# Byte places of the matmul operands, and the order of two steps on POOL, in a hybrid encoder layer

## The chip, the cores and the metric

The kernel runs on one core of a Trainium2 chip. The metric is the device time of one execution in microseconds (us), median over runs. TensorE (PE) multiplies, ScalarE (ACT), VectorE (DVE) and GpSimd (POOL) compute elementwise, SyncE (SP) issues DMAs.

## What is computed

One layer over 512 tokens of width 1024: a half feed-forward block, a token mixer, a second half feed-forward block, each with a normalisation in front, then a last normalisation.

```python
x = x + 0.5 * g1 * swiglu(mod(rms_norm(x)), w1, w3, w2)      # 1024 -> 2816 -> 1024
h = mod(rms_norm(x)); z = h @ w_in                             # mixer: HGRN2 heads and RG-LRU blocks
x = x + g2 * concat(hgrn2(z), rglru(z)) @ w_out
x = x + 0.5 * g3 * swiglu(mod(rms_norm(x)), w1', w3', w2')
return rms_norm(x)
def swiglu(h, w1, w3, w2): return (silu(h @ w1) * (h @ w3)) @ w2
```

## The kernel before

Tokens lie transposed in SBUF, features on the partitions. Every float32 operand is split into an upper part (rounded to fp32r by ACT) and a lower part (the rest, by a subtraction on DVE), and each product is made of three matmuls: upper weights on upper tokens, upper weights on lower tokens, lower weights on upper tokens (`three`, and the loop in `product`). Upper weights are `whi`, lower ones `wlo`.

**Wide units.** A unit is 8 weight blocks of 128x128, 4 KB in each partition. SP loads it into `raw`, ACT copies it to `whi`, DVE subtracts into `wlo`. Each of its matmuls has 512 columns. The down projections of the feed-forward blocks run this way with tokens `ghi2`, `glo2`, and so do the mixer's projections, and the first 8 units of each feed-forward block (tokens `hhi`, `hlo`).

**Groups.** The other 18 of 22 column blocks of w1 and w3 are computed in 36 groups (18 in each feed-forward block, `PAIRS` = 9 times s = 0 and 1) by a Strassen-like scheme: instead of 8 block products there are 7 (`PRODUCTS`), each of 4 x 3 = 12 matmuls with 256 columns, so 84 matmuls per group. I number the groups g = 2j + s. Products 0, 5 and 6 read tokens `hhi`/`hlo`, products 1 to 4 sums of tokens kept in `forms`. Weights of products 0 to 3 are in `hi4`/`lo4`, which lie over `whi`/`wlo`; those of 4 to 6 in `hix`/`lox`.

The weights of a group come about like this:
- SP (`load_group`, L454) loads two quarters of the weights, each written twice, into `sraw_a[s]` ("base loads"; `sraw_a[1]` is `raw`), when DVE has subtracted the first two parts of group g-2. Then, when all four parts of g-2 are done, it loads a third quarter into `sraw_b[s]` (L457).
- POOL (`add_fourth`, L506) waits for the base loads and issues a DMA that adds the fourth quarter onto two of the four copies ("adding transfer").
- POOL (`long_sums`) waits for that DMA, adds `xs[0]` (L514), then `xs[1]` (L517).
- ACT (`group_upper`, L720) copies part 0, 1 (`sraw_a`), 2 (`xs`) and 3 (`sraw_b`) to the upper weights, each when TensorE has finished the products of the previous group that used this place.
- DVE (`group_lower`, L1377) subtracts in the same order. Part 1 also waits for the first sum of POOL, since its end frees `sraw_a` for SP's next load. Between the parts, in the fixed order of its queue, DVE evacuates the previous group's sums (L1385 to L1403) and multiplies the gates (L1410, L1412).
- TensorE (`product`, L1979 to L1981) waits for part 0 ahead of product 0, part 1 ahead of product 2, part 2 ahead of product 4, part 3 ahead of product 6.

POOL's queue is in order: adding transfer of g, sums of g, adding transfer of g+1, sums of g+1, and so on (`up_sums`).

**Places.** `sb` and `at` put tiles one behind the other, rounded to 64 bytes. The first tile begins at byte 16512 of each partition, which is 128 modulo 256. By the sizes of the tiles `hhi`, `hlo`, `raw`, `whi`, `wlo` begin at 128 modulo 256 too (and with them `hi4`, `lo4`, and `yhi`, `ylo` of the mixer), while `arena` and all that is counted from it (`ghi2`, `glo2`, `forms`, `hix`, `lox`, and the mixer's tiles) begin at 192. All strides inside a tile are multiples of 256 bytes, so the relation holds for each matmul.

Of the kernel before, what the change touches and what calls it, by code (L numbers as in the profile page):

```python
# [22 lines left out]
F32R = mybir.dt.float32r  # L23
# [4 lines left out]
P = 128  # L28
HALF = P // 2
T = 512  # L30
# [8 lines left out]
N_MOD = 9  # L39
EPS = 1e-6  # L40
UNIT = KD * P
HALF_UNITS = KF // 2
PAIR_UNITS = HALF_UNITS - 4
LEVELS = (64, 32, 16, 8, 4, 2, 1)
# [53 lines left out]
def build(nc, xt, wu, ws, wada, c_rows, vecs_in, bd_in, consts_in, out):  # L98
    with ExitStack() as ctx:
        place = [nc.sbuf_base + (-nc.sbuf_base) % 64]  # L100

        def at(name, shape, dt, offset):

            n = int(np.prod(shape[1:])) * (1 if dt == U8 else 4)
            return nc.alloc_sbuf_tensor_at(name, shape, dt, offset=offset), offset + (n + 63) // 64 * 64

        def sb(name, shape, dt=F32):
            t, place[0] = at(name, shape, dt, place[0])
            return t

        def sem(name):
            return ctx.enter_context(nc.semaphore(name))

# [3 lines left out]
        hhi = sb("hhi", [P, KD, T], F32R)  # L117
        hlo = sb("hlo", [P, KD, T], F32R)
        raw = sb("raw", [P, 2, UNIT])
        whi = sb("whi", [P, 2, UNIT], F32R)  # L120
        wlo = sb("wlo", [P, 2, UNIT], F32R)
        vecs = sb("vecs", [P, N_VEC])
        ident = sb("ident", [P, P])
        ones = sb("ones", [P, P])
# [11 lines left out]
        nomh, omk = small[:, 120:128], small[:, 128:136]  # L136
        half_b, half_gain = small[:, 56:72], small[:, 72:73]
        modt = sb("modt", [P, KD])
        arena = place[0]

        off = arena
        early, off = at("early", [P, BLOCKS, KD, T], F32, off)
        raw2, off = at("raw2", [P, 2, UNIT], F32, off)
# [5 lines left out]
        off = arena  # L149
        ghi2, _ = at("ghi2", [P, KF, T], F32R, off)  # L150
        forms, off = at("forms", [P, 4, 2, KD // 2 * HT], F32R, off + PLAIN * T * 4)
# [4 lines left out]
        csr, _ = at("csr", [P, D], F32, off - 4 * D)  # L156
        ada = tuple(at(f"ada{i}", [P, D], F32, a)[0] for i, a in
                    enumerate((off - 12 * D, off - 8 * D, off, off + 4 * D)))
        hix, off = at("hix", [P, 3, T], F32R, off)
        lox, off = at("lox", [P, 3, T], F32R, off)  # L160
        sraw_a = (sraw_a0, raw[:].rearrange("p u (q n) -> p (u q) n", q=2))
        sraw_b = (sraw_b0, sraw_b1)
        g2_at = off
        g2, off = at("g2", [P, KF, T], F32, g2_at)
        glo2, _ = at("glo2", [P, KF, T], F32R, g2_at)
        h32, t_at = at("h32", [P, KD, T], F32, g2_at + PLAIN * T * 4)
# [16 lines left out]
        off = arena  # L183
# [203 lines left out]

            return psum[:, 5 - 4 * s:7 - 4 * s, :].rearrange("p b (h t) -> p (b h) t", h=2)

        hi4 = whi[:].rearrange("p u (q n) -> p (u q) n", q=2)  # L390
        lo4 = wlo[:].rearrange("p u (q n) -> p (u q) n", q=2)
        h_left, h_right = h32[:, :, 0:HT], h32[:, :, HT:T]

        def tokens(i, k):
# [91 lines left out]
        def _(pool):  # L486
# [16 lines left out]
            def add_fourth(j, s):  # L503

                pool.wait_ge(base_loaded[s], 32 * j + 32)
                pool.dma_start(sraw_a[s][:, 1:3, :], twice(quarter(j, s, 3)), accum_op=ALU.add  # L506
                               ).then_inc(sum_loaded[s], 16)
# [11 lines left out]
            def up_sums(n):  # L519

                j0 = PAIRS * n
                add_fourth(j0, 0)
                long_sums(j0, 0)
                add_fourth(j0, 1)
                with pool.Fori(j0, j0 + PAIRS - 1) as j:
                    long_sums(j, 1)
                    add_fourth(j + 1, 0)
                    long_sums(j + 1, 0)
                    add_fourth(j + 1, 1)
                long_sums(j0 + PAIRS - 1, 1)  # L530

            def load_row(r):
# [50 lines left out]
        def _(act):  # L583
# [119 lines left out]
            def group_upper(j, s, part):  # L703

                if opens(j) and s == 0:
                    if part < 2:
                        act.wait_ge(unit_used, DOWN_AT[j // PAIRS] - 1 + part)
                else:
                    act.wait_ge(prod_done, 14 * j + (7 * s - (5, 3, 1, 0)[part]))
                if part == 3:  # L710
                    act.wait_ge(third_loaded[s], 16 * j + 16)
                if part < 2:
                    act.wait_ge(sum_loaded[s], 16 * j + 16)
                    src, dst = sraw_a[s][:, 2 * part:2 * part + 2, :], hi4[:, 2 * part:2 * part + 2, :]
                elif part == 2:
                    act.wait_ge(xs_done, 4 * j + (2 * s + 2))
                    src, dst = xs[:], hix[:, 0:2, :]
                else:
                    src, dst = sraw_b[s][:], hix[:, 2, :]
                nc.scalar.activation(dst, src, ACT.Copy).then_inc(shi_done, 1)  # L720
# [400 lines left out]
        def _(dve):  # L1121
# [244 lines left out]
            def group_lower(j, s, part):  # L1366

                dve.wait_ge(shi_done, 8 * j + (4 * s + part + 1))
                if part == 1:
                    dve.wait_ge(xs_done, 4 * j + (2 * s + 1))  # L1370
                if part < 2:
                    src, up, dst = (t[:, 2 * part:2 * part + 2, :] for t in (sraw_a[s], hi4, lo4))
                elif part == 2:
                    src, up, dst = xs[:], hix[:, 0:2, :], lox[:, 0:2, :]
                else:
                    src, up, dst = sraw_b[s][:], hix[:, 2, :], lox[:, 2, :]
                nc.vector.tensor_tensor(dst, src, up, ALU.subtract).then_inc(slo_done, 1)  # L1377
# [525 lines left out]
        def _(pe):  # L1903
# [48 lines left out]
            def product(j, s, i):  # L1952
# [19 lines left out]
                if i == 6:  # L1972
                    pe.wait_ge(p1_copied, 2 * j + (s + 1))
                dst = sum_bank(i, s)
                up, low = (hi4[:, i, :], lo4[:, i, :]) if i < 4 else (hix[:, i - 4, :], lox[:, i - 4, :])
                for k in range(KD // 2):
                    a, b = up[:, k * P:(k + 1) * P], low[:, k * P:(k + 1) * P]
                    rhi, rlo = tokens(i, k)
# [505 lines left out]
```

## Time and profile before

| | |
|---|---|
| median of 3 runs | 1018.17 us (1016.67 to 1020.95) |
| profiled execution | 1020.35 us |
| its span, first to last instruction | 1018.6 us |
| TensorE busy | 991.1 us |
| granted TensorE clock, mean | 0.997 |
| groups of the first feed-forward block | about 76 to 258 us |
| groups of the second | about 707 to 884 us |

The profile is one execution. Busy time of TensorE counts overlapping matmuls once; since matmuls are pipelined, the time that one costs is read from the distance between two starts, not from its length. Instructions that only wait or issue count as idle, except POOL's own issue of a DMA.

### The profile page before, as it was taken

How to read it: one execution, taken by the hardware profiler on the slowest of the kernel's cores; microseconds unless marked ns; L12 is line 12 of the kernel's file. 1: busy time of each engine (PE TensorE's matmuls, PEld its weight loads, DVE VectorE, ACT ScalarE, POOL GpSimd, SP SyncE). 2: the span in 40 equal slices, each digit the busy share in tenths (PEclk: the TensorE clock that was granted, in tenths of full speed). 3: DMA queues.
4: the chain of work that ended last, by engine and by line, in shares of the span. 5: the costliest groups of instructions: out<-in, count | busy, mean ns of one | idle time of the engine just before them, and what ended most of it. 6: DMA issues, size and time to landing. Idle time of an engine off the chain costs nothing.

```text
span 1018.6 us, 18633 instructions
## 1 busy us (share of the span) xinstructions
PE 991.1 (97%) x6974; PEld 862.8 (85%) x6974; DVE 751.4 (74%) x1039; ACT 502.9 (49%) x690; POOL 225.7 (22%) x191
## 2 busy tenths in 40 slices
PE   7999999999999999999999989999999999999997
PEld 5779999999888888776677767878999999988887
DVE  5777777887787858879899995566877877683334
ACT  5545444444333124588977973465444444433221
POOL 0023444453112301100100000202444443200100
PEclk9999999999999999999999999999999999999999
DMA  9556657665788736622221202235677676552322
GB/s 351 213 174 155 197 149 212 167 195 152 270 289 311 280 134 218 215 98 73 74 84 42 83 23 77 90 120 138 173 211 189 180 205 167 186 179 90 103 83 83
DMA packets 64470, 163.79 MB, mean 161 GB/s; under 512 B 5696, under 2 KB 8016, under 8 KB 64416
## 3 DMA queue, kind: packets, MB, share of 16 engines
q1 hardware_dynamic: 44720, 110.79, 30.6%
q0 software_dynamic: 18416, 50.16, 19.9%
q10 hardware_dynamic: 1280, 2.10, 0.9%
q8 instruction: 36, 0.59, 0.2%
q14 instruction: 18, 0.15, 0.0%
HBM read 158.83 MB, written 2.10 MB: 158 GB/s over the span
## 4 chain that ended last, share of the span: by engine, by line
PE 81%; DMA 5%; ACT 5%; DVE 5%; issue 2%; SPq 1%; DVEq 0%; POOLq 0%; ACTq 0%
PE psum L1907 15%; PE psum L1909 15%; PE psum L1908 14%; PE psum L1979 10%; PE psum L1981 10%; PE psum L1980 10%; DMA sraw_a<-ws 4%; DMA raw<-wu 1%; PE psum L2284 1%; PE psum L2278 1%; ACT whi L589 1%; PE psum L2208 1%; DVE wlo L1377 1%; PE psum L2210 1%; PE psum L2209 1%
## 5 line engine op out<-in xcount | busy, mean ns | idle before, releaser
L589 ACT ACTIVATE whi<-raw 128x1024 fp32r<-128x1024 f32 x92 | 97.3, 1057 | 221.1 <-PE psum L1909 209.5
L1125 DVE TENSOR_TENSOR wlo<-raw,whi 128x1024 fp32r<-128x1024 f32 x94 | 118.1, 1256 | 117.3 <-ACT whi L589 116.9
L1909 PE MATMUL psum<-ghi,wlo 128*128 128x512 f32 (+2 forms) x384 | 144.0, 375 | 0.0
L1908 PE MATMUL psum<-glo,whi 128*128 128x512 f32 (+2 forms) x384 | 143.3, 373 | 0.0
L1907 PE MATMUL psum<-ghi,whi 128*128 128x512 f32 (+2 forms) x384 | 143.2, 373 | 0.0
L1907 PE MATMUL psum<-hhi,whi 128*128 128x512 f32 x320 | 129.2, 404 | 2.0 <-DVE wlo L1125 1.3
L1909 PE MATMUL psum<-hhi,wlo 128*128 128x512 f32 x320 | 125.2, 391 | 0.0
L1908 PE MATMUL psum<-hlo,whi 128*128 128x512 f32 x320 | 125.0, 391 | 0.0
L1979 PE MATMUL psum<-forms,whi 128*128 128x256 f32 x432 | 121.2, 281 | 0.0
L1980 PE MATMUL psum<-forms,whi 128*128 128x256 f32 x432 | 120.7, 279 | 0.0
L1981 PE MATMUL psum<-forms,wlo 128*128 128x256 f32 x432 | 120.7, 279 | 0.0
L1377 DVE TENSOR_TENSOR wlo<-sraw_a,whi 128x1024 fp32r<-128x1024 f32 x36 | 56.7, 1594 | 48.8 <-ACT whi L720 47.4
L1908 PEld LDWEIGHTS psum<-glo,whi 128*128 128x128 f32 x384 | 72.1, 188 | 13.8
L1907 PEld LDWEIGHTS psum<-ghi,whi 128*128 128x128 f32 x384 | 72.2, 188 | 13.1
L1909 PEld LDWEIGHTS psum<-ghi,wlo 128*128 128x128 f32 x384 | 72.3, 188 | 12.2
L1981 PEld LDWEIGHTS psum<-forms,wlo 128*128 128x128 f32 x432 | 81.4, 188 | 0.0
L1979 PEld LDWEIGHTS psum<-forms,whi 128*128 128x128 f32 x432 | 81.3, 188 | 0.0
L1980 PEld LDWEIGHTS psum<-forms,whi 128*128 128x128 f32 x432 | 81.1, 188 | 0.0
L1979 PE MATMUL psum<-hhi,hix 128*128 128x256 f32 x288 | 80.0, 278 | 0.0
L1980 PE MATMUL psum<-hlo,hix 128*128 128x256 f32 x288 | 79.8, 277 | 0.0
L1981 PE MATMUL psum<-hhi,lox 128*128 128x256 f32 x288 | 79.8, 277 | 0.0
L1907 PEld LDWEIGHTS psum<-hhi,whi 128*128 128x128 f32 x320 | 60.1, 188 | 22.1 <-issue 5.5
(272 smaller groups left out, 2344.7 us busy)
## 6 DMA issues: line engine op xcount, KB each, us to landing
raw<-wu SPq DMA_DIRECT2D x96, 512.0 KB, 3.4
ada<-wada POOLq DMA_DIRECT2D x56, 512.0 KB, 5.1
sraw_a<-ws SPq DMA_DIRECT2D x36, 512.0 KB, 5.9
raw<-ws SPq DMA_DIRECT2D x36, 512.0 KB, 6.0
sraw_b<-ws SPq DMA_DIRECT2D x36, 256.0 KB, 4.3
sraw_a<-ws POOLq DMA_DIRECT2D x18, 512.0 KB, 6.1
raw<-ws POOLq DMA_DIRECT2D x18, 512.0 KB, 6.0
early<-wada SPq DMA_DIRECT2D x16, 512.0 KB, 15.3
```

The source lines that it names most:

```text
L589: nc.scalar.activation(whi[:, slot, :], raw[:, slot, :], ACT.Copy).then_inc(hi_done, 1)
L1125: nc.vector.tensor_tensor(wlo[:, slot, :], raw[:, slot, :], whi[:, slot, :], ALU.subtract).then_inc(lo_done, 1)
L1377: nc.vector.tensor_tensor(dst, src, up, ALU.subtract).then_inc(slo_done, 1)
L1907: nc.tensor.matmul(dst, a, rhi, start=start, stop=False)
L1908: nc.tensor.matmul(dst, a, rlo, start=False, stop=False)
L1909: return nc.tensor.matmul(dst, b, rhi, start=False, stop=stop)
L1979: nc.tensor.matmul(dst, a, rhi, start=(k == 0 and i < 6), stop=False, skip_group_check=(i == 6))
L1980: nc.tensor.matmul(dst, a, rlo, start=False, stop=False, skip_group_check=(i == 6))
L1981: ins = nc.tensor.matmul(dst, b, rhi, start=False, stop=(k == KD // 2 - 1), skip_group_check=(i == 6))
L2208: nc.tensor.matmul(dst, hhi[:, k, cc], a, start=(k == 0), stop=False)
L2209: nc.tensor.matmul(dst, hhi[:, k, cc], b, start=False, stop=False)
L2210: ins = nc.tensor.matmul(dst, hlo[:, k, cc], a, start=False, stop=(k == KD - 1))
```

## The change

There are two parts. First, places: `whi` and `wlo` get 256 spare bytes per unit (`GAP`), and the group weights get tiles of their own over the same bytes, the upper ones 64 bytes and the lower ones 192 bytes further; `hix` and `lox` are likewise put at 64 and 192 bytes past 128 modulo 256; `arena` and `g2_at` are rounded up to 128 modulo 256, so that `forms`, `ghi2` and `glo2` begin there. Second, order: in `up_sums` the adding transfer of group g+1 is put ahead of the long sums of group g. The number and the shapes of the instructions stay.

```diff
+LINES = 256
+PHASE = 128
+GAP = LINES // 4
+        def on_line(offset, phase):
+            return offset + (phase - offset) % LINES
-        whi = sb("whi", [P, 2, UNIT], F32R)
-        wlo = sb("wlo", [P, 2, UNIT], F32R)
+        whiw, wlow, hi4w, lo4w = ([], [], [], [])
+        for name, group, wide, grouped, by in (("whi", "hi4", whiw, hi4w, 64), ("wlo", "lo4", wlow, lo4w, 192)):
+            first = on_line(place[0], PHASE)
+            grouped.append(at(group, [P, 2, UNIT + GAP], F32R, first + by)[0])
+            place[0] = first
+            wide.append(sb(name, [P, 2, UNIT + GAP], F32R))
+            place[0] += by
+        whi, wlo = whiw[0][:, :, 0:UNIT], wlow[0][:, :, 0:UNIT]
+        hi4, lo4 = (w[0][:, :, 0:UNIT].rearrange("p u (q n) -> p u q n", q=2) for w in (hi4w, lo4w))
-        arena = place[0]
+        arena = on_line(place[0], PHASE)
-        hix, off = at("hix", [P, 3, T], F32R, off)
-        lox, off = at("lox", [P, 3, T], F32R, off)
+        hix, off = at("hix", [P, 3, T], F32R, on_line(off, PHASE + 64))
+        lox, off = at("lox", [P, 3, T], F32R, on_line(off, PHASE + 192))
-        g2_at = off
+        g2_at = on_line(off, PHASE)
                 j0 = PAIRS * n
                 add_fourth(j0, 0)
+                add_fourth(j0, 1)
                 long_sums(j0, 0)
-                add_fourth(j0, 1)
                 with pool.Fori(j0, j0 + PAIRS - 1) as j:
+                    add_fourth(j + 1, 0)
                     long_sums(j, 1)
-                    add_fourth(j + 1, 0)
+                    add_fourth(j + 1, 1)
                     long_sums(j + 1, 0)
-                    add_fourth(j + 1, 1)
                 long_sums(j0 + PAIRS - 1, 1)
```

## Rows read from the trace of the kernel before

**Rows 1.** The page, part 1: busy time, share of the span, instructions.

```profile
PE 991.1 (97%) x6974; PEld 862.8 (85%) x6974; DVE 751.4 (74%) x1039; ACT 502.9 (49%) x690; POOL 225.7 (22%) x191
```

**Rows 2.** Windows: us, busy us and instructions of each engine, clock, DMA share, GB/s.

```profile
106.00:150.00 44.00, 40.51 (x344) 40.12 (x343) 31.85 (x37) 17.66 (x24) 18.87 (x13) 1.00 0.63 167
150.00:248.00 98.00, 98.00 (x837) 97.97 (x836) 80.56 (x92) 45.72 (x61) 46.71 (x31) 1.00 0.64 174
740.00:870.00 130.00, 130.00 (x1111) 130.00 (x1110) 103.05 (x120) 62.34 (x80) 59.69 (x41) 1.00 0.69 185
```

**Rows 3.** Waits of TensorE, 76 to 150 us: total, times, longest.

```profile
PE psum L1979 <- DVE wlo L1377: 3.5, 2, 1.9
```

**Rows 4.** TensorE in time (start, duration): starts of groups 1, 7; a later group's products.

```profile
86.19 0.28 PE L1979 MATMUL psum<-hhi,whi 128*128 128x256 f32 x1
...
149.39 0.28 PE L1979 MATMUL psum<-hhi,whi 128*128 128x256 f32 x1
...
775.95 0.28 PE L1979 MATMUL psum<-hhi,whi 128*128 128x256 f32 x1
...
777.38 0.28 PE L1979 MATMUL psum<-forms,whi 128*128 128x256 f32 x1
...
781.63 0.28 PE L1979 MATMUL psum<-forms,hix 128*128 128x256 f32 x1
...
783.06 0.29 PE L1979 MATMUL psum<-hhi,hix 128*128 128x256 f32 x1
...
784.44 0.28 PE L1979 MATMUL psum<-hhi,hix 128*128 128x256 f32 x1
...
785.80 0.28 PE L1979 MATMUL psum<-hhi,whi 128*128 128x256 f32 x1
```

**Rows 5.** TensorE in time, 512 columns: 12 matmuls apart, then 9 apart.

```profile
635.63 0.39 PE L1907 MATMUL psum<-yhi,whi 128*128 128x512 f32 x1
...
638.35 0.39 PE L1907 MATMUL psum<-yhi,whi 128*128 128x512 f32 x1
...
299.75 0.39 PE L1907 MATMUL psum<-ghi,whi 128*128 128x512 f32 x1
...
301.81 0.39 PE L1907 MATMUL psum<-ghi,whi 128*128 128x512 f32 x1
```

**Rows 6.** SP's base loads and POOL's adding DMA of the same group, in time.

```profile
843.64 0.94 SPq L454 DMA_DIRECT2D sraw_a<-ws  x2
...
849.54 1.20 POOL L506 DMA_DIRECT2D sraw_a<-ws  x1 [0.19 <-issue]
...
709.68 0.96 SPq L454 DMA_DIRECT2D sraw_a<-ws  x2
...
715.30 1.20 POOL L506 DMA_DIRECT2D sraw_a<-ws  x1
...
79.03 0.97 SPq L454 DMA_DIRECT2D sraw_a<-ws  x2
...
85.34 1.20 POOL L506 DMA_DIRECT2D sraw_a<-ws  x1 [0.70 <-DMA sraw_a<-ws]
```

**Rows 7.** DVE, SP and POOL in time, 814 to 846 us.

```profile
822.53 1.23 DVE L1377 TENSOR_TENSOR wlo<-sraw_a,whi 128x1024 fp32r<-128x1024 f32 x1 [1.37 <-ACT whi L720]
...
823.93 0.94 SPq L454 DMA_DIRECT2D sraw_a<-ws  x2
...
826.64 1.29 POOL L514 TENSOR_TENSOR xs<-raw 128x512 f32<-128x512 f32 x1 [4.90 <-DMA raw<-ws]
...
830.39 1.20 POOL L506 DMA_DIRECT2D sraw_a<-ws  x1 [0.75 <-issue]
```

**Rows 8.** Line L506, 815 to 850 us: its DMAs, issue to landing.

```profile
DMA to landing us min/median/max: 5.9/6.0/6.1
```

**Rows 9.** POOL and DVE in time, two pairs that start close together.

```profile
497.86 1.64 POOL L564 TENSOR_TENSOR tmp<-ra 128x512 f32<-128x512 f32 x1 [10.48 <-ACT ra L929]
...
497.92 0.68 DVE L1701 TENSOR_TENSOR qk<-w 128x512 f32<-128x512 f32 x1
...
799.66 1.29 POOL L517 TENSOR_TENSOR xs<-xs,sraw_b 128x512 f32<-128x512 f32 x1
...
799.96 2.08 DVE L1377 TENSOR_TENSOR wlo<-sraw_a,whi 128x1024 fp32r<-128x1024 f32 x1 [1.53 <-ACT whi L720]
```

More of the change, by code:

```diff
@@ L388, in three_banks @@
             return psum[:, 5 - 4 * s:7 - 4 * s, :].rearrange("p b (h t) -> p (b h) t", h=2)
-        hi4 = whi[:].rearrange("p u (q n) -> p (u q) n", q=2)
-        lo4 = wlo[:].rearrange("p u (q n) -> p (u q) n", q=2)
         h_left, h_right = h32[:, :, 0:HT], h32[:, :, HT:T]
@@ L713, in group_upper @@
                     act.wait_ge(sum_loaded[s], 16 * j + 16)
-                    src, dst = sraw_a[s][:, 2 * part:2 * part + 2, :], hi4[:, 2 * part:2 * part + 2, :]
+                    src, dst = sraw_a[s][:, 2 * part:2 * part + 2, :], hi4[:, part]
                 elif part == 2:
@@ L1371, in group_lower @@
                 if part < 2:
-                    src, up, dst = (t[:, 2 * part:2 * part + 2, :] for t in (sraw_a[s], hi4, lo4))
+                    src, up, dst = sraw_a[s][:, 2 * part:2 * part + 2, :], hi4[:, part], lo4[:, part]
                 elif part == 2:
@@ L1974, in product @@
                 dst = sum_bank(i, s)
-                up, low = (hi4[:, i, :], lo4[:, i, :]) if i < 4 else (hix[:, i - 4, :], lox[:, i - 4, :])
+                up, low = (hi4[:, i // 2, i % 2], lo4[:, i // 2, i % 2]) if i < 4 else (hix[:, i - 4, :], lox[:, i - 4, :])
                 for k in range(KD // 2):
```

## Prediction, made blind

> **What bounds the kernel now.** I read the page's busy times first, then windows by stage, then the waits of TensorE, then single matmuls by their start times. TensorE is busy 97% of the span [rows 1], so only what stands under it can move the end. The windows [rows 2] say where it is not full: in the group products of the second feed-forward block 130.00 of 130 us are busy, in those of the first 98.00 of 98 us from 150 on, but only 40.51 of 44 us between 106 and 150. That hole is the wait of the products for `wlo`, 3.5 us in two pieces [rows 3]. By the starts of group 1 (86.19) and group 7 (149.39) [rows 4] six periods took 63.2 us, where six of 9.85 (below) are 59.1: 4.1 us lost in all. Everything else is a full TensorE at granted clock 1.00 (the 2.4 GHz level), so what counts there is the distance between two matmul starts.
>
> **Starts of one group (84 matmuls) [rows 4].** From 775.95 to 785.80 is 9.85 us, and there are 36 groups. It divides unevenly though all matmuls have one shape: product 0 (`hhi` on `whi`) takes 1.43 us for 12, products 1 to 3 (`forms` on `whi`) 4.25 us for 36 (118 ns each), product 4 (`forms` on `hix`) 1.43 us (119), product 5 1.38 with its start-up, and product 6 (`hhi` on `hix`) 1.36 us for 12 (113). The layout tells them apart. Before, tokens in `hhi` and weights in `whi` both begin at 128 modulo 256 bytes, `forms` and `hix` at 192. So: weights at the tokens' own place cost 119 to 120 ns, weights 192 (= 64 short) behind them 118, weights 64 behind them 113. For 512 columns: at the same place 2.72 us for 12 (226.7 ns), weights 192 behind 2.06 us for 9 (229 ns) [rows 5].
>
> **Part 1, the places.** After the change all tokens (`hhi`, `hlo`, `forms`, `ghi2`, `glo2`) begin at 128, the upper group weights (`hi4`, `hix`) 64 behind them, the lower ones (`lo4`, `lox`) 192 behind, the wide weights at 128. Two of three matmuls of every product use the upper weights, one the lower. Taking the row for each: (2 x 113.3 + 118) / 3 = 114.9 ns, 84 x 114.9 = 9.65 us per group, 0.20 us less. If TensorE stays the bound that is 36 x 0.20 = 7.2 us. Mixing an upper weight at 64 and a lower one at 192 in one product is in no row. Bounds: all at 120 ns gives 10.08 us (+8.2 us in all); below, all at 113 gives 9.49 us (-13 us), and as the kind of stall is unknown I let it go to 108 ns, 9.07 us. I take 114.9. The second half of the feed-forward blocks (`ghi2` on `whi`, 512 columns, 960 matmuls) goes from 192 behind to the same place: 960 x 2.3 ns = 2.2 us saved; its 192 half-width ones go from 118 to 120 ns, 0.4 us lost: net -1.8 us. The copies on ACT and DVE keep their shapes and cost nothing new; the mixing stage moves all its arena tiles by the same 192 bytes forward (64 back modulo 256) and its matmuls keep their pairs' relations, so zero.
>
> By the Trainium skill (SBUF — State Buffer, "Who interferes with whom") TensorE has two independent read ports and never waits for anyone, which would make the places worth nothing. The trace disagrees: 113 against 118 to 120 ns for one shape [rows 4].
>
> **Part 2, the order on POOL.** The adding transfer of group g+1 now stands ahead of the long sums of group g. Nothing is added; what moves are one DMA issue of 1.20 us and the wait in front of it, for the base quarters of g+1. Queued behind that wait are now the two sums of g (`xs`), and behind them: DVE's second subtraction of g (it waits for the first sum before it frees the buffer), DVE's evacuations of g-1 behind that, ACT's copy into `hix`, and SP, which loads the base quarters of g+2 only when DVE's second subtraction of g is done. This closes a loop that takes one group, where the old one took two:
> - base loads issued by SP until the adding DMA issues: 5.90 us where 2.5 us of an adding transfer ran beside them (843.64 to 849.54), 5.62 us where it was 1 us (709.68 to 715.30), 6.31 us in the first block with little beside them (79.03 to 85.34) [rows 6];
> - its issue 1.20, the first sum 1.29, DVE's subtraction 1.23, DVE's end to SP's issue 0.17 (823.76 to 823.93) [rows 7], and hand-overs of about 0.13: together 4.02 us.
> An adding transfer lands 6.0 us after its issue [rows 8], and the next base load would be issued 4.02 us after it, so 2.0 us lie side by side: between the rows 5.62 and 5.90, so 5.76. The loop is 9.78 us in the second block; in the first, where loads are slower (6.31), about 6.0 + 4.02 = 10.0. Bounds: 5.62 + 4.02 = 9.64 below for both; above 6.31 + 4.02 = 10.33, and 10.6 for the first block as a guess for crowded loads.
>
> So the supply, 9.78 and 10.0, is longer than the 9.65 that the products would need, and it sets the period. In the old order POOL was idle in most of this time: the first sum ran at 826.64 and the adding DMA only at 830.39 [rows 7]; the new order puts the sum behind that DMA, 5 us later, and that uses up the slack in which it lay hidden.
>
> The gain of the order: the adding DMA no longer waits for the sums ahead of it, so the two holes go. In place of 171.7 us for the 17 periods of the first block (17 x 9.85 + 4.1) stand 17 x 10.0 = 170.0, -1.7 us. The second block has 17 x 9.78 = 166.3 instead of 167.5, -1.2 us. Two things at the head of each block I only allow for: the weights made ahead of the first product give a lead that the slower supply first uses up, and the first group's sums now stand behind group 1's adding DMA. They have opposite signs and are under 1 us each; together -0.3 us.
>
> **The sum.** -1.8 - 1.7 - 1.2 - 0.3 = -5.0 us on the profiled execution's 1020.35 (span 1018.6): 1015.4. That execution lies 2.2 us above the median of 1018.17, so the median goes to 1013.2; I say 1013.
>
> **The port of DVE and POOL.** In the new order DVE's second subtraction and POOL's second sum are released by the same event, the end of the first sum. They exclude each other: POOL's sum began at 799.66 and DVE's subtraction 0.30 later took 2.08 instead of 1.23 us; at 497.86 POOL began 0.06 ahead of DVE's 497.92, and it was POOL that waited: it took 1.64 us against 1.29 for a sum of that size [rows 7, 9], while DVE was done in 0.68. Both would start within a tenth of a microsecond of the event, which is nearer to the second pair, so I expect DVE to win. The Trainium skill's rule (same page and section: the pair of ports is a lock, held by whoever issues first) fits the first pair; in the second POOL's start is the earlier by the records.
>
> **Rivals.** (a) DVE loses that race each time. The subtraction then ends one sum (1.29 us) later, inside the one-group loop: 11.1 and 11.3 us per group. It costs 17 x 1.25 + 17 x 1.45 - 4.1 - 1.8 = +40 us, 1058. It decides from the point where the loop passes 9.85, which is at once; against it stands the second pair of [rows 9]. A milder form has the same place and sign: the base loads stay at 6.3 us in both blocks, loop 10.33 to 10.6: 17 x 0.48 + 17 x 0.75 - 4.1 - 1.8 = +15 us, 1033.
> (b) The supply keeps up: loop 9.6 in both blocks, products at 9.65 or below. The holes go and all of part 1 is earned: -7.2 - 4.1 - 1.8 = -13 us, 1005. If the mixed places give 108 ns and base loads turn round 0.5 us sooner than any row shows, the loop is 9.1 us and the time 1018 - 34 x 0.75 - 6 = 987; I give that little.
> (c) The places do nothing in the mix (120 ns, 10.08 us per group), which puts TensorE back as the bound with supply beneath it: 36 x 0.22 - 4.1 - 1.8 = +2 us, 1020. The Trainium skill's rule that TensorE never waits, which the rows speak against, would give periods of 9.85 with the holes gone at best, 1014: inside the forecast.
>
> **Chances.** Forecast (1006 to 1020) 0.45; (a) in both forms 0.23; (b) 0.22; (c) 0.10. A measurement here can tell about 0.5%, 5.1 us, from no change. Faster by more: (b) and under half of the forecast, as its middle is right at the bound: 0.42. Slower by more: (a) and a bit of (c): 0.25. Within: 0.33. The range runs from 1000, inside (b), to 1034, the milder (a), and leaves out 0.2.
>
> **What would show it.** A steady group's starts: 84 x 114.9 ns where TensorE is not waiting, with products 5 and 6 no longer the fast ones; matmuls of 512 columns on `ghi2` at 226.7 ns. The periods of groups: 9.65 means the supply keeps up, 9.8 to 10.0 with a small idle piece per group, ahead of product 2 or 4, means the loop. The waits list shows POOL's adding DMA waiting for the base loads and its first sum right behind it, ACT's `hix` waiting for POOL's `xs`. DVE's second subtraction of a group takes 1.23 us if it wins the port, over 2 if it loses. The prediction is wrong if base loads land well under 5 us after their issue, or if mixed places cost under 113 ns and the loop follows.

## The result, and the profile after

The kernel became slower: 1034.11 us median of 4 (1032.53 to 1035.98) against 1017.85 for the kernel before on the same chip, ratio 1.0163, 95% interval 1.0142 to 1.0184. The forecast was 1013, its range 1000 to 1034. The profiled execution took 1032.53 us, its span 1030.8, which is 12.2 us more than the span of before. Groups are numbered as before; "period" is the time from one group's first matmul to the next one's.

The page, part 1, answers [rows 1]:

```profile
PE 988.1 (96%) x6974; PEld 854.8 (83%) x6974; DVE 743.7 (72%) x1039; ACT 496.7 (48%) x690; POOL 226.7 (22%) x191
```

TensorE is busy 3.0 us less in a span 12.2 us longer: it now waits. The windows of [rows 2] show where (window, its length, then busy us and instructions of PE, PEld, DVE, ACT, POOL, granted clock, DMA share, GB/s):

```profile
106.00:150.00 44.00, 41.82 (x359) 40.92 (x358) 30.26 (x37) 17.45 (x24) 21.95 (x15) 1.00 0.69 172
150.00:248.00 98.00, 93.06 (x799) 91.36 (x799) 71.67 (x87) 43.60 (x60) 45.98 (x29) 1.00 0.67 172
740.00:870.00 130.00, 123.31 (x1056) 120.90 (x1055) 94.68 (x112) 52.43 (x73) 62.47 (x39) 1.00 0.69 175
```

The hole between 106 and 150 has become smaller, from 3.49 us to 2.18. In return the two stretches that were full have lost 4.94 of 98 and 6.69 of 130 us. The clock is granted in full in all three, so it has no part in this. The waits of the second block (707 to 885 us; who waited for whom: total us, times, longest):

```profile
ACT hix L732 <- POOL xs L529: 72.0, 16, 6.8
...
DVE lo L1389 <- POOL xs L526: 21.2, 11, 3.8
...
PE psum L1991 <- DVE lo L1389: 9.3, 8, 1.8
```

Before, TensorE waited only twice, 3.5 us in all, and only in the first block [rows 3]. Now it waits 8 times in the second block for a subtraction on DVE (7 times, 7.8 us, in the first), DVE waits for POOL's first sum, and ACT's copy into `hix` for the second.

By the starts of the groups the 17 periods of the first block went from 171.7 to 176.2 us and those of the second from 167.5 to 177.9 us; all outside the two blocks' periods gave back 2.9 us. Sum: +4.6 + 10.4 - 2.9 = +12.1 us, the span's difference within rounding.

TensorE in time (start us, duration), 12 matmuls of 512 columns apart, answers [rows 5]:

```profile
299.54 0.39 PE L1919 MATMUL psum<-ghi,whi 128*128 128x512 f32 x1
...
302.26 0.39 PE L1919 MATMUL psum<-ghi,whi 128*128 128x512 f32 x1
```

2.72 us for 12 is 226.7 ns, as forecast. And the group matmuls are 113.3 ns apart in all seven products, not 114.9.

**The loop.** One turn that runs as forecast (SP, POOL and DVE in time: start us, duration, in brackets the idle time before it and what ended it; answers [rows 6] and [rows 7]):

```profile
160.74 0.94 SPq L466 DMA_DIRECT2D sraw_a<-ws  x2
...
166.87 1.20 POOL L518 DMA_DIRECT2D sraw_a<-ws  x1 [5.15 <-DMA sraw_a<-ws]
167.65 1.76 POOL L526 TENSOR_TENSOR xs<-raw 128x512 f32<-128x512 f32 x1
169.48 2.34 POOL L529 TENSOR_TENSOR xs<-xs,sraw_b 128x512 f32<-128x512 f32 x1
...
169.44 1.23 DVE L1389 TENSOR_TENSOR lo<-raw,hi 128x1024 fp32r<-128x1024 f32 x1 [1.50 <-POOL xs L526]
...
170.84 0.94 SPq L466 DMA_DIRECT2D raw<-ws  x2
```

Base loads to adding DMA 6.13 us, adding DMA to the next base loads 3.97 us. The end of the first sum releases both the second subtraction on DVE and the second sum on POOL. DVE starts 0.04 us ahead: its 1.23 us is undisturbed, and the second sum pays (2.34 us).

**What was not forecast.** The very next turn (ACT, POOL, DVE, TensorE and SP in time):

```profile
175.14 0.85 ACT L750 ACTIVATE silu<-csum 128x768 f32<-128x768 f32 x1 [1.44 <-DVE csum L1415]
...
176.15 2.00 ACT L732 ACTIVATE hi<-sraw_a 128x1024 fp32r<-128x1024 f32 x2
...
176.25 1.20 POOL L518 DMA_DIRECT2D raw<-ws  x1 [4.44 <-DMA raw<-ws]
177.03 1.75 POOL L526 TENSOR_TENSOR xs<-sraw_a 128x512 f32<-128x512 f32 x1
...
177.24 2.64 DVE L1389 TENSOR_TENSOR lo<-sraw_a,hi 128x1024 fp32r<-128x1024 f32 x1 [1.53 <-ACT hi L732]
...
179.93 0.39 PE L1991 MATMUL psum<-hhi,hi 128*128 128x256 f32 x1 [1.29 <-DVE lo L1389]
...
182.28 0.94 SPq L466 DMA_DIRECT2D sraw_a<-ws  x2
```

Here DVE's first subtraction starts 0.21 us behind POOL's first sum, takes 2.64 us instead of 1.22, TensorE waits 1.29 us for it, and the second subtraction now comes behind POOL's second sum. From adding DMA to the next base loads it is 6.03 us instead of 3.97. I call this a meeting. It happens in groups 6, 10, 12, 14, 23, 25, 28, 30 and 34. In the seven even ones its root is two queues up: `hix` waits for the late second sum, so DVE's last evacuation is late, so ACT's SiLU of `csum` is late (175.14), and the next group's first upper part stands behind that SiLU in ACT's queue. In the two odd ones, 23 and 25, no SiLU stands there. The first subtraction follows DVE's own gate products without a pause (before group 23 the last of them starts at 759.88 and the subtraction at 760.75).

### The profile page after: what moved, and what is told of

It is laid out like the page before. It is cut to its first block, busy times and chain, and to the rows that moved or that the text cites. A ratio compares the mean times of both kernels' runs of the same rounds, so it can differ in the third digit from the quotient of the medians.

```text
span 1030.8 us, 18633 instructions
## 1 busy us (share of the span) xinstructions
PE 988.1 (96%) x6974; PEld 854.8 (83%) x6974; DVE 743.7 (72%) x1039; ACT 496.7 (48%) x690; POOL 226.7 (22%) x191
## 4 chain that ended last, share of the span: by engine, by line
PE 55%; DMA 11%; DVE 10%; ACT 7%; issue 7%; POOL 6%; SPq 2%; POOLq 0%; DVEq 0%; ACTq 0%
PE psum L1919 15%; PE psum L1921 14%; PE psum L1920 14%; DMA sraw_a<-ws 6%; DVE lo L1389 5%; POOL xs L526 4%; DMA raw<-ws 4%; POOL xs L529 2%; PE psum L1991 2%; PE psum L1993 2%; PE psum L1992 2%; DMA early<-wada 2%; ACT hi L732 1%; SPq L466 1%; PE psum L2296 1%
## 5 line engine op out<-in xcount | busy, mean ns | idle before, releaser
L1137 DVE TENSOR_TENSOR wlo<-raw,whi 128x1024 fp32r<-128x1024 f32 x94 | 117.9, 1255 | 115.2 <-ACT whi L601 114.9
L1991 PE MATMUL psum<-forms,hi 128*128 128x256 f32 x432 | 120.0, 278 | 4.1 <-DVE lo L1389 4.1
L1993 PE MATMUL psum<-forms,lo 128*128 128x256 f32 x432 | 119.3, 276 | 0.0
L1992 PE MATMUL psum<-forms,hi 128*128 128x256 f32 x432 | 119.3, 276 | 0.0
L732 ACT ACTIVATE hix<-xs 128x1024 fp32r<-128x1024 f32 x36 | 38.3, 1063 | 156.4 <-POOL xs L529 147.2
L1389 DVE TENSOR_TENSOR lo<-sraw_a,hi 128x1024 fp32r<-128x1024 f32 x36 | 64.9, 1817 | 38.4 <-ACT hi L732 25.4
L1991 PEld LDWEIGHTS psum<-forms,hi 128*128 128x128 f32 x432 | 81.1, 188 | 5.2 <-DVE lo L1389 5.2
L1992 PEld LDWEIGHTS psum<-forms,hi 128*128 128x128 f32 x432 | 81.1, 188 | 0.0
L1993 PEld LDWEIGHTS psum<-forms,lo 128*128 128x128 f32 x432 | 81.1, 188 | 0.0
```

Source lines behind the costliest of these rows:

```text
L1137: nc.vector.tensor_tensor(wlo[:, slot, :], raw[:, slot, :], whi[:, slot, :], ALU.subtract).then_inc(lo_done, 1)
L1991: nc.tensor.matmul(dst, a, rhi, start=(k == 0 and i < 6), stop=False, skip_group_check=(i == 6))
L1992: nc.tensor.matmul(dst, a, rlo, start=False, stop=False, skip_group_check=(i == 6))
L1993: ins = nc.tensor.matmul(dst, b, rhi, start=False, stop=(k == KD // 2 - 1), skip_group_check=(i == 6))
```

## The experiments

Theory: the one-group loop is there with about the forecast length, and the rest of the loss are the meetings. Rivals: the places cost something; the port race is lost; the order costs through the loop's length alone.

**e1_places: the places alone, POOL's old order.**

```diff
                 with pool.Fori(j0, j0 + PAIRS - 1) as j:
-                    add_fourth(j + 1, 0)
                     long_sums(j, 1)
+                    add_fourth(j + 1, 0)
```

(and likewise for the two other transfers that the change had moved, as in the kernel before)

> The changed kernel with POOL's order put back: the places alone. Theory (the loss comes from the order alone, the places only help): matmuls of the groups at 113.2 ns apart, so 9.51 us per group where TensorE is fed, and 226.7 ns for 512 columns; the old two-group supply loop (base load 7.5, add 6.2, ACT and DVE 5) then limits some groups to 9.6 to 9.8 us. Sum: -3 to -6 us in the second block, -1 to -3 in the first, -2 in the down projections: 1006 to 1012 us, holes in the first block remain. Rival 1 (the places also cost something, by the copies into shifted tiles or by the arena's shift): 1018 or more. Rival 2 (the supply follows entirely): 36 x 0.34 + 2 = 14 us less, 1004.

Measured: 1007.92 us, ratio 0.9906 (0.9871 to 0.9940). This is in the expected range. The places alone are worth 1% and the order costs more than they give. The 17 periods of the second block are 9.52 us = 84 x 113.3 ns (the first one 9.54). In time, starts of groups 24 and 25:

```profile
757.39 0.28 PE L1991 MATMUL psum<-hhi,hi 128*128 128x256 f32 x1
...
766.91 0.28 PE L1991 MATMUL psum<-hhi,hi 128*128 128x256 f32 x1
```

In the first block the periods before groups 4 and 5 are 12.01 and 11.27 us, so the hole of [rows 3] is still there. The first is a wait of 2.3 us. The second has no wait: it is the clock behind it (window, as above):

```profile
116.70:120.00 3.30, 3.24 (x15) 3.24 (x16) 3.27 (x5) 1.88 (x3) 2.27 (x2) 0.53 0.09 13
```

Only 15 matmuls in 3.3 us at a granted clock of 0.53, which is nearly the lower level. The lines of POOL's adding DMAs from 76 to 130 us in this kernel, and then in the kernel after:

```profile
DMA to landing us min/median/max: 5.9/6.2/8.8
```

```profile
DMA to landing us min/median/max: 5.7/6.1/6.3
```

**e2_order: the order alone, on the kernel before.**

```diff
                 add_fourth(j0, 0)
+                add_fourth(j0, 1)
                 long_sums(j0, 0)
-                add_fourth(j0, 1)
                 with pool.Fori(j0, j0 + PAIRS - 1) as j:
+                    add_fourth(j + 1, 0)
                     long_sums(j, 1)
-                    add_fourth(j + 1, 0)
```

(and likewise for the second transfer of the loop, as in the change)

> The kernel before with POOL's new order: the order alone. Theory (the one-group loop through the sums, with DVE's first subtraction held up by POOL's first sum in every second group, sets the period whatever TensorE needs): periods of groups alternate between about 9.9 and 11, mean 10.4 to 10.5, and the time is that of the changed kernel plus the 3 us that the places save outside the groups: 1033 to 1038 us. Rival (the loss needs the faster matmuls or the new places as well): periods of 9.85, 1014 to 1020 us.

Measured: 1039.54 us, ratio 1.0205 (1.0165 to 1.0245), 1.5 us above the expected range. In the first block the 17 periods take 179.6 us, in the second 178.2, many of them 9.95 and 11.3 in turn. With the places of before the products alone need 9.85, and the loop is still above that. So the loss is all in the order, and the gain all in the places. The two do not simply add: the places save 9.6 us under the old order (1017.54 to 1007.92) and 5.4 under the new one (1039.54 to 1034.11), where the loop and not the products sets the period.

**e3_silu: the kernel after, with ACT's SiLU of `csum` behind the next group's first two upper parts.** It takes away what makes the first subtraction late, and leaves POOL's order.

```diff
                 for part in range(4):
+                    if s and part == 2:
+                        second_silu(j)
                     group_upper(j + s, 1 - s, part)
```

(cut: `second_silu(j)` holds the last two lines of `group_silu`)

> The changed kernel with one step on ACT moved: the silu of the csum part is done behind the first two copies of the next group, not ahead of them. Theory: in every second group DVE's first subtraction comes late because ACT's copy stood behind this silu, meets POOL's first sum at the port, and DVE's first two subtractions take 2.6 and 2.3 us instead of 1.2 each; without it a pair of groups needs about 19 us instead of 21: the time falls by 20 to 30 us to 1004 to 1014, and DVE's subtractions of parts 0 and 1 have a mean near 1.25 us. Rival (the one-group loop of base load, adding DMA, sum and subtraction is the limit by its own length, as predicted 9.8 to 10.0 us per group): 1015 to 1022. Rival 2 (the order costs by something else, for instance the late second sum): within 3 us of the changed kernel.

Measured: 1028.46 us, ratio 1.0098 (1.0075 to 1.0121). My expectation of 1004 to 1014 missed, and so did both rivals, since the loop's length and the meetings that remain act together. In the first block no first subtraction meets a sum any more, and its 17 periods take 172.0 us (10.12 each) instead of 176.2: the loop without meetings, at the forecast's 10.0. In the second block five odd groups still meet (23, 25, 27, 29, 33), since there DVE's gate products stand in front (DVE in time, POOL, then DVE again):

```profile
775.89 0.95 DVE L1430 TENSOR_TENSOR g<-silu,csum 128x768 f32 x1
...
776.37 1.20 POOL L518 DMA_DIRECT2D sraw_a<-ws  x1 [4.62 <-DMA sraw_a<-ws]
777.15 1.75 POOL L526 TENSOR_TENSOR xs<-raw 128x512 f32<-128x512 f32 x1
...
776.76 3.24 DVE L1395 TENSOR_TENSOR lo<-raw,hi 128x1024 fp32r<-128x1024 f32 x1
```

The last line is DVE's next instruction, the first subtraction of group 25. It starts 0.39 us ahead of the sum's record, and yet takes 3.24 us. The sum's record begins inside that of POOL's own DMA issue (777.15 against 777.57 for its end).

**e4_between: the adding DMA between the two sums.**

```diff
+                    first_sum(j, 1)
                     add_fourth(j + 1, 0)
-                    long_sums(j, 1)
+                    second_sum(j, 1)
```

(and likewise for the loop's second transfer; cut: `long_sums` is split into its two sums)

> The changed kernel with the adding transfer of the next group put between POOL's first and second sum. The first sum, which frees the buffer for the next base loads, is then not behind the wait for the base loads; only the second sum is. Theory (what costs is that the first sum is behind that wait): the time is near that of the places alone, 1006 to 1014 us. Rival (the second sum behind the wait, and with it hix and product 4, is what costs): 1020 or more, with TensorE waiting ahead of product 4.

Measured: 1007.37 us, ratio 0.9887 (0.9850 to 0.9923), as expected. The first sum of a group stands ahead of the wait for the next group's base loads again, so the chain doesn't close in one group. The 17 periods take 163.8 us in the first block (e1: 166.8) and 166.4 in the second (e1: 161.9): it closes the hole and opens small ones. Second subtractions meet the second sum here too and take up to 3.46 us (group 11), but outside a chain of one group that costs little.

**e7_between_first: that order in the first three pairs of the first block, the old one elsewhere.**

```diff
+                    if between:
+                        first_sum(j, s)
+                        add_fourth(j + s, 1 - s)
+                        second_sum(j, s)
+                    else:
+                        long_sums(j, s)
+                        add_fourth(j + s, 1 - s)
```

(cut: the loops that call it)

> The new places with POOL's old order, but in the first three pairs of groups of the first block the adding transfer stands between the two sums. A try at a faster version: with the places alone the first block lost 4.9 us at groups 2, 4 and 5, and with the transfer between the sums everywhere it lost under 2 there, but 4.6 in the second block. Theory: 2 to 3 us under the places alone, 1004 to 1006, every period 9.52 from group 6 on. Rival: the crowding of the loads only moves to later groups, 1007 to 1009.

Measured: 1006.43 us, ratio 0.9894 (0.9874 to 0.9914); periods 163.1 and 162.3 us. It beats both kernels, but the intervals don't tell it from e1, and it is 0.4 us above the expected range. In the trace the hole is gone: the longest wait of TensorE in the first block is 0.3 us instead of e1's 2.3, no low clock follows, and the periods before groups 4 and 5 are 9.52.

**e8_apart: e3 with DVE's gate products between the first and the second subtraction of the next group.**

```diff
                 group_lower(j + s, 1 - s, 0)
+                if s == 0 and not opens(j):
+                    gated(n, j - 1)
                 group_lower(j + s, 1 - s, 1)
...
-                if s:
-                    gated(n, j)
```

> The kernel of the moved silu (changed kernel, new order on POOL), in which DVE also does its first subtraction of the odd group ahead of the gate products of the pair before, not behind them. Theory (two costs in the new order: the one-group loop by its length, 9.9 to 10.1 us, and the meetings of DVE's first subtraction with POOL's first sum, about 2 us each): no subtraction of part 0 or 1 above 1.3 us in the steady part, no period above 10.5, mean 9.9 to 10.1 in both blocks; time 1017 to 1023, still not under the kernel before. Rival (the meetings are all of the loss): periods near 9.52, 1004 to 1009. Rival 2 (the meetings cost nothing by themselves): within 3 us of the moved silu's 1028.

Measured: 1031.09 us, ratio 1.0126 (1.0101 to 1.0151); periods 10.42 and 10.48 on average. My expectation missed. No first subtraction meets a sum now, but the gate product does, and so the second subtraction is late (DVE and POOL in time, group 27):

```profile
803.82 1.22 DVE L1395 TENSOR_TENSOR lo<-raw,hi 128x1024 fp32r<-128x1024 f32 x1
804.95 0.41 DVE L1428 TENSOR_TENSOR g<-silu,psum 128x256 f32 x1
805.28 3.07 DVE L1430 TENSOR_TENSOR g<-silu,csum 128x768 f32 x1
...
805.79 1.75 POOL L526 TENSOR_TENSOR xs<-raw 128x512 f32<-128x512 f32 x1
807.61 1.90 POOL L529 TENSOR_TENSOR xs<-xs,sraw_b 128x512 f32<-128x512 f32 x1
...
808.28 2.31 DVE L1395 TENSOR_TENSOR lo<-raw,hi 128x1024 fp32r<-128x1024 f32 x1
```

The gate product takes 3.07 us, the second subtraction behind it 2.31. It doesn't matter which DVE instruction meets the first sum: whichever is ahead of the second subtraction passes the delay into the loop.

**e9_gates_after: e3 with the gate products behind the second subtraction.** Then neither the gate product nor a first subtraction should stand where a first sum starts.

```diff
                 group_lower(j + s, 1 - s, 0)
                 group_lower(j + s, 1 - s, 1)
+                if s == 0 and not opens(j):
+                    gated(n, j - 1)
                 middle_sums(j, s)
...
-                if s:
-                    gated(n, j)
```

> The kernel after, with ACT's SiLU of csum moved behind the first two upper parts of the next group (as in e3_silu) and both gate products of DVE moved behind its second subtraction of the next pair's first group. So nothing stands ahead of DVE's first two subtractions in any group, and no long DVE instruction stands between them either (in e8_apart the gates did). Theory (two terms: the loop of one group, and the meetings of DVE's first subtraction with POOL's first sum on top of it): no first or second subtraction is over 1.4 us where it starts at or ahead of its sum, the periods are 9.9 to 10.1 us in both blocks (the loop alone, as e3_silu's first block showed 10.12 with few meetings), 17 periods of the second block take 169 to 172 us, and the time is 1017 to 1023. Rival 1 (the meetings are all of the loss and the loop is shorter than the products): periods 9.5 to 9.6, 1005 to 1009. Rival 2 (a meeting comes back in another place, since the gates now delay the evacuation and through hix the sums): periods stay at 10.4, 1028 to 1031.

Measured: 1023.61 us, ratio 1.0043 (1.0013 to 1.0073), 0.6 us above the expected range. The meetings are gone: first and second subtractions take 1.22 to 1.23 us in groups 6 to 16 and 21 to 34. From adding DMA to the base loads that these second subtractions release it is 3.93 to 3.98 us. A turn (SP, POOL, DVE):

```profile
820.89 0.94 SPq L466 DMA_DIRECT2D raw<-ws  x2
...
826.37 1.21 POOL L518 DMA_DIRECT2D raw<-ws  x1 [4.51 <-DMA raw<-ws]
827.14 1.75 POOL L526 TENSOR_TENSOR xs<-sraw_a 128x512 f32<-128x512 f32 x1
...
828.93 1.23 DVE L1395 TENSOR_TENSOR lo<-sraw_a,hi 128x1024 fp32r<-128x1024 f32 x1 [1.40 <-POOL xs L526]
...
830.33 0.94 SPq L466 DMA_DIRECT2D sraw_a<-ws  x2
```

The period is 9.72 us on average over 14 of the first block and 9.83 over 14 of the second, below the 9.9 to 10.1 I expected, and above e1's 9.52. The other three periods of each block are long (10.48, 13.54 and 11.28; 10.39, 10.59 and 15.11), and that is partly this kernel's own doing: the gate product behind the second subtraction holds a bank (TensorE in time, start of group 3, then the waits of both blocks: total, times, longest):

```profile
109.59 0.38 PE L1997 MATMUL psum<-hhi,hi 128*128 128x256 f32 x1 [2.76 <-DVE g L1428]
...
PE psum L1997 <- DVE g L1428: 4.1, 4, 2.8
...
PE psum L1997 <- DVE g L1428: 5.4, 5, 2.8
```

In the 28 steady periods, too, TensorE's waits end with the gate product and not with a weight (ahead of groups 9, 11, 13, 15, 23, 25, 29 and 33, 0.10 to 1.01 us). The gate product stands right behind the second subtraction, so it keeps the loop's pace. What the loop would cost with the gates elsewhere was not measured.

Behind the wait at group 3 the clock falls, behind the one of 2.82 us at group 21 it does not:

```profile
109.60:113.00 3.40, 3.40 (x18) 3.40 (x19) 3.37 (x4) 2.23 (x4) 0.67 (x1) 0.57 1.05 317
...
743.00:747.00 4.00, 4.00 (x38) 4.00 (x37) 3.97 (x6) 3.19 (x5) 0.22 (x1) 1.00 0.85 273
```

So the time of e9 is the loop plus these waits. Its steady turns, not its time, give the loop's length.

**The places by themselves.** Four kernels with POOL's old order (two of them the same), which differ in the bytes by which weights lie behind the tokens. Each ran once, so the distances in the traces count here, not the times.

```diff
-for name, group, wide, grouped, by in (("whi", "hi4", whiw, hi4w, 64), ("wlo", "lo4", wlow, lo4w, 192)):
+for name, group, wide, grouped, by, wide_by in (("whi", "hi4", whiw, hi4w, UP, WIDE_UP), ("wlo", "lo4", wlow, lo4w, LOW, WIDE_LOW)):
```

UP, LOW, WIDE_UP, WIDE_LOW are 128, 128, 64, 192 in p1; 192, 64, 128, 128 in p2 and p4; 64, 64, 192, 64 in p3; `hix` and `lox` go with UP and LOW.

> Old order. Group weights, upper and lower, 128 bytes behind the tokens' place; wide upper weights 64 and wide lower weights 192 behind it. No row has a distance of 128. Theory (only a weight at the tokens' own place modulo 256 bytes, or the upper weights 192 behind, costs; the rest is 113 ns): 113 ns per group matmul; for 512 columns 220 to 227 ns by the same gain of 6 ns. Rival (the distance counts in steps, each dearer): 116 or more at 128; 227 or more for 512 columns.

Measured: 1025.63 us. Matmuls of the groups 118.7 ns apart on average, period 9.97; 512 columns 231.9 ns. That is the rival for both.

> Old order. The group weights' places exchanged: upper 192 behind, lower 64 behind the tokens' place. Theory (the upper weights decide, since two of three loads are theirs): 116 to 118 ns per group matmul, 9.8 us a group. Rival (what counts is that upper and lower weights differ in place): 113 ns as in the changed kernel.

Measured: 1025.07 us, and within one execution both distances (starts of groups 16, 17, 30 and 31):

```profile
229.71 0.28 PE L1990 MATMUL psum<-hhi,hi 128*128 128x256 f32 x1
...
239.23 0.28 PE L1990 MATMUL psum<-hhi,hi 128*128 128x256 f32 x1
...
826.99 0.28 PE L1990 MATMUL psum<-hhi,hi 128*128 128x256 f32 x1
...
836.98 0.28 PE L1990 MATMUL psum<-hhi,hi 128*128 128x256 f32 x1
```

9.52 and 9.99 us, 113.3 and 118.9 ns. The change comes between groups 19 and 20, where TensorE idles 1.10 us. So the rival's 113 held for a part of one execution, and in the rest the distance was above the theory's 118.

> The same kernel as p2_192_and_64 once more (order on POOL as before, upper group weights 192 bytes behind the tokens' place, lower ones 64 behind, wide ones 128 behind). There the matmuls of the groups were 113.3 ns apart until an idle piece of 1.3 us in the second block, and 118.9 from there on. If the idle piece switches a state of TensorE's reads, the change comes again behind the first idle piece of about this length, in the same or another group; if it was an accident of that execution, it does not come again and all groups stay at 113.3 (then the time is about 1008). If it is bound to the place in the program, it comes at the same group.

Measured: 1020.41 us, and the same kernel does it the other way about (starts of groups 16, 17, 30 and 31):

```profile
237.04 0.28 PE L1990 MATMUL psum<-hhi,hi 128*128 128x256 f32 x1
...
247.03 0.28 PE L1990 MATMUL psum<-hhi,hi 128*128 128x256 f32 x1
...
825.57 0.28 PE L1990 MATMUL psum<-hhi,hi 128*128 128x256 f32 x1
...
835.09 0.28 PE L1990 MATMUL psum<-hhi,hi 128*128 128x256 f32 x1
```

9.99 in the whole first block, 9.52 in the whole second. None of what I had offered (the same group, the next idle piece, no change at all) fits.

> The order on POOL as before; both group weights 64 bytes behind the tokens' place, wide upper weights 192 behind, wide lower ones 64 behind. For the distance between matmul starts: if only an upper and a lower weight at 64 and 192 (one each) give 113.3 ns, both at 64 give 118 or more in a group; if what counts is that no weight of the three matmuls lies at the tokens' own place, they give 113.3 as one product of the kernel before did with its upper weights. Wide matmuls (512 columns) at 229 to 232 ns against 226.7 at the same place. Time 1007 to 1012 in the first case 1005 to 1010 plus 960 x 3 ns for the wide ones; over 1020 if groups go to 118.

Measured: 1026.22 us. 113.4 ns in groups 0 to 5, 117.8 ns from group 6 to the end. The 512 columns changed too: 233.3 ns in the first block's down projection (12 matmuls from 301.64 to 304.44 us), 229.2 in the second's. Group 6 follows small idle pieces too, but those in front of groups 2 and 4 changed nothing. With these places the distance is a state that TensorE keeps over many groups, and the places alone don't fix it. With upper weights 64 and lower ones 192 behind (the change's) it was about 113.3 in every group of all seven kernels that had them, each seen in its one profiled execution.

## Why the prediction was wrong

**The places: right in sign, too small.** The step averaged two rows, (2 x 113.3 + 118) / 3 = 114.9 ns. It measured 113.3 and a fed group 9.52 us instead of 9.65. The average over rows of other pairs was no estimate for the mix; why the mix runs at 113.3 is open, and p2 to p4 show that a pair of places need not have one distance. The lower end of 108 ns did cover it. The 512 columns came as forecast. By the Trainium skill (SBUF — State Buffer, "Who interferes with whom") TensorE never waits for another engine, and places don't appear there. It may still hold between engines, but one instruction shape ran at 113.3 and at 118.9 ns in p2 and p4 with the same bytes, so the rule gives no distance.

**The loop: right in kind and size.** It was to be 5.76 us (base loads to adding DMA) + 4.02 (adding DMA to next base loads) = 9.78. In the kernel after the first term is 5.67 us on average over groups 5 to 16 and 5.71 over 22 to 34, and the second is 3.95 to 3.97 where nothing meets. In e9, without meetings, the first is 5.82 and 5.87, and a whole turn is 9.79 and 9.83 us on average (groups 7 to 16, 22 to 34). The 10.0 for the first block was 0.2 too much.

**The missing term: the step that failed.** The prediction's part on the port of DVE and POOL asked only whether the *second* subtraction and the *second* sum, which one event releases, collide. It put the *first* subtraction against POOL's first sum at nothing, without a reason. In the kernel after that pair meets in nine groups.

In the old order the first sum always came first. DVE's first subtraction began at least 1.03 us behind it, in every group of the kernel before, and took 1.2 to 1.6 us in all but four. Group 8 of the kernel before, then group 31's first subtraction:

```profile
156.62 1.29 POOL L514 TENSOR_TENSOR xs<-sraw_a 128x512 f32<-128x512 f32 x1 [5.22 <-DMA sraw_a<-ws]
157.65 1.34 DVE L1377 TENSOR_TENSOR wlo<-sraw_a,whi 128x1024 fp32r<-128x1024 f32 x1 [2.70 <-ACT whi L720]
...
830.38 1.21 DVE L1377 TENSOR_TENSOR wlo<-raw,whi 128x1024 fp32r<-128x1024 f32 x1
```

In group 31 the sum of [rows 7] begins at 826.64 and the first subtraction at 830.38. The prediction itself moved that sum 5 us later, to 831.6, which is where the first subtraction ends, but did not look there. The subtraction of 799.96 in [rows 9] is a first subtraction too, and it met a second sum already in the old order. In the new order the first subtraction is ahead of the sum in most groups, by 0.6 to 3.4 us. Where it is late, because the late sum delays `hix`, the evacuations, the SiLU and with it the first upper part, or because gate products stand in front, the two meet.

The second part of the loop takes 3.96 us in most steady turns, and 6.02 in the eight turns behind a meeting (the ninth meeting, in group 34, has no base loads behind it): 8 x 2.06 = 16.5 us of loop time. A part comes back: the adding DMA issues 5.40 us behind those late base loads, against 5.83 in the other turns, 8 x 0.43 = 3.4 us. In the first turns of each block it is 5.14 to 5.24 us, since in groups 1, 2, 18, 19 and 20 the second subtraction loses its race: 5 x 1.2 = 6 us more, which the lead in weights partly hides.

That is rival (a) with another instruction: POOL does win a port race, in nine groups, and at the first pair instead of the second. Its milder form named 10.33 to 10.6 us a period and 1033 us; the periods are 10.37 and 10.47, but through meetings, not through base loads at 6.3 us. It was a right number with a wrong cause.

**The race at the second pair: right in the steady groups.** DVE starts 0.04 us ahead and wins there. In groups 1, 2, 19 and 20 POOL's second sum starts 0.02 us ahead and the subtraction takes 2.34 to 2.35 us; why the hand-over falls the other way there is open. The Trainium skill (same page and section) says that whoever issues first gets the pair and the other blocks; all pairs at the second sum in the kernel after agree. But by the records alone several first pairs disagree: in groups 12, 23, 25 and 34 of the kernel after DVE started 0.06 to 0.33 us ahead and lost, and in group 25 of e3 it started 0.39 us ahead and lost 2.0 us.

**The holes of the first block: wrong cause.** I had put them down to the adding DMA waiting for the sums ahead of it, and counted -1.7 us. In e1 the adding DMA of group 2 took 8.8 us to land, and that of group 4 8.0, while the next group's base loads ran beside them and took 8.8 and 8.2 us from the first issue to the last landing. That is crowding of transfers, by the trace alone: no run takes it away and leaves the rest. The change did end it (at most 6.3 us there), and e4 and e7 end it as well, with the transfer only one sum earlier than in the old order.

**The sum, term by term.** Forecast against measured, by the profiled executions: outside the group periods -1.8 against -2.9 us; first block 170.0 against 176.2; second 166.3 against 177.9. The miss in the two blocks is 17.8 us, of the size of the missing term (16.5 us of meetings less the 3.4 that come back, and up to 6 of lost races, less what slack takes up). In e3 and e9, which take meetings away in part or wholly, the time falls to 1028.46 and 1023.61. e9 is still 15.7 us over e1's 1007.92, and 18.2 us by the profiled executions (1025.01 against 1006.78). Of these 18.2 us, 7.2 are in its 28 steady periods (0.20 and 0.31 above 9.52), 14.2 in the three long periods of each block (6.7 and 7.5) and 1.7 outside the blocks. The 4.9 us by which e1's own first block is above 9.52 a period go off. What of e9's long periods belongs to the order and what to its own moved gates, with the clock behind one of them, was not measured apart.

So of the 26.2 us between e1 and the kernel after, 10.5 go when the meetings go (e9), though e9 adds waits of its own. The steady loop's length over 9.52 costs about 7 us in e9, where the waits end with the gate product behind the loop; the rest lies mostly at the starts of the blocks. That the order is the cause is shown (e1, e2), and that the meetings are a part of it (e3, e9); the shares are estimates. The kernel before ran at 1017.2 to 1017.9 beside all these runs.

## What to carry to other kernels

When a step is moved behind another on one queue, follow not only the instructions that wait for it but also the next group's instructions behind those on their queues: a delay of 5 us that is "hidden" at its own place can come out two queues further as a late start, and can push the moved step onto an instruction that it used to be ahead of. Then ask of each pair on DVE and POOL where in the new order they fall in time, not only those that one event releases. In this kernel nearly every second subtraction of e1 met a POOL operation and took 2.3 us, with periods of 9.52 all the same; what made a meeting dear was its place inside a chain of one group.

A chain that takes one group and is 9.8 us long has no slack against products of 9.5. When something else is made faster (here the places), it is this slack that has to be counted again.

## What the runs showed of the hardware

- The distance between fp32r matmuls of 256 columns was 113.3, about 118 or up to 120 ns (product 0 of the kernel before). It goes with the bytes modulo 256 at which tokens and weights begin (e1 against the kernel before), but for some places it is a state: the same kernel ran whole blocks at 113.3 and whole blocks at 118.9. For 512 columns it was 226.7 with both at one place, 229.0 with weights 192 behind (before), 233.3 and then 229.2 with 192 and 64 (p3), 231.9 with 64 and 192 (p1), and 232.3 to 233.3 with 128 (p2, p4). What sets and changes the state stays open.
- Where a sum follows POOL's own DMA issue, the port is taken earlier than the sum's record says: DVE subtractions that started 0.27 to 0.40 us ahead of the first sum's record (e3, groups 23 to 29), and 0.50 us ahead (e2, groups 6 and 10), still lost; those 0.57 us ahead (e3, groups 13 and 31) and 0.60 us ahead (the kernel after, group 8) won. Ahead of the second sum in e4 0.61 us still lost (group 11) and 0.65 won (group 31). The sum's record is then 1.75 us long instead of 1.29. Whether the DMA issue or the sum holds the port is not shown.
- An idle piece can cost nearly as much again behind it. After waits of 1.95 us (p2), 2.3 (e1) and 2.76 (e9) the granted clock of the next 3.3 to 3.4 us was 0.64, 0.53 and 0.57, between the levels of 1.2 and 2.4 GHz, and matmuls were up to 213 ns apart; in e1 the period behind the wait is 1.75 us over 9.52. The length of the wait alone does not decide it. After waits of 2.29 and 2.82 us in e9's second block and 2.30 us in p3 the clock stayed at 1.00, and in e4 it fell (0.51 from 584.7 to 588.2 us) behind waits of only 1.17 and 0.96 us in the mixer, whose like left it at 1.00 in the kernel before. The window of p2:

```profile
745.50:748.90 3.40, 3.40 (x19) 3.40 (x20) 3.35 (x4) 1.85 (x3) 2.22 (x2) 0.64 0.14 17
```
